# Cached-key scores by VectorE beside the prompt's attention, a split output projection, and an earlier routing table

## The reference

```
q, k = rope(rmsnorm(q)), rope(rmsnorm(k))            # 8 heads x 64
s = index_scores(qi, ki, wi); idx = top_k(s, 64)     # causal, per query
logits = (q . k[idx]) / 8;  p = softmax(logits)      # sample rows: k from cache_k[page_table] and the new key
y_att = p . v[idx]
y_ssm = gelu(y) * sigmoid(gelu(y) @ w_glu)
x = x + concat([y_ssm, y_att]) @ w_out
x = x + swiglu(rmsnorm(x)); x = x + pool_mixer(...); x = x + moe(top 2 of 8)
```

## Time and profile before

| | us |
|---|---|
| median of 3 runs | 1623.99 (1620.77 to 1626.13) |
| the profiled execution, device time | 1629.38 |
| the profiled execution, span in the trace | 1627.2 |
| PE busy | 1556.8 (96%) |
| DVE busy | 1256.8 (77%) |
| ACT busy | 987.8 (61%) |
| POOL busy | 115.0 (7%) |

### The profile page before, as it was taken

How to read it: one execution, slowest core, us unless ns; L and a number is a source line. 1 busy time by engine, 2 the same in 40 slices (tenths; PEclk the granted TensorE clock), 3 DMA queues, 4 the chain that set the end, 5 groups by cost and what they waited for, 6 DMA issues and landing times.

```text
span 1627.2 us, 23220 instructions
## 1 busy us (share of the span) xinstructions
PE 1556.8 (96%) x7648; PEld 1249.3 (77%) x7648; DVE 1256.8 (77%) x1670; ACT 987.8 (61%) x1305; POOL 115.0 (7%) x157
## 2 busy tenths in 40 slices
PE   6998988989999689999999999999999999999998
PEld 5664564789999567888888888888888888888886
DVE  8978820155544669989989889989988988988986
ACT  5111442144443157777777777778778778777774
POOL 1377510000000000000000000000000000000000
PEclk9998879999999889999999999999999999999999
DMA  6401125345445429999999999999998998999992
GB/s 226 154 26 53 56 84 153 107 142 179 156 143 169 157 78 332 373 343 332 365 348 325 369 357 319 364 357 319 369 371 303 367 372 311 362 367 335 345 358 98
DMA packets 212891, 420.83 MB, mean 259 GB/s; under 512 B 10233, under 2 KB 56469, under 8 KB 212572
## 3 DMA queue, kind: packets, MB, share of 16 engines
q1 hardware_dynamic: 211542, 414.37, 71.5%
q10 hardware_dynamic: 622, 3.45, 0.5%
q0 software_dynamic: 672, 2.32, 0.4%
HBM read 417.50 MB, written 3.07 MB: 258 GB/s over the span
## 4 chain that ended last, share of the span: by engine, by line
PE 83%; DVE 3%; ACT 1%; issue 1%; DMA 1%; SPq 1%; DVEq 0%; ACTq 0%
PE bank L1281 19%; PE bank L1280 19%; PE bank L1276 19%; PE bank L1139 3%; PE bank L1136 3%; PE bank L1140 3%; PE bank L1119 2%; PE bank L1301 2%; PE bank L1151 1%; PE bank L1155 1%; PE bank L1154 1%; PE bank L1239 1%; PE bank L866 1%; PE bank L1316 1%; PE bank L1056 1%
## 5 line engine op out<-in xcount | busy, mean ns | idle before, releaser
L2093 DVE TENSOR_TENSOR split<-raw_w,split 128x1024 fp32r<-128x1024 f32 x672 | 787.5, 1219 | 36.0 <-ACT split L1645 32.5
L1645 ACT ACTIVATE split<-raw_w 128x1024 fp32r<-128x1024 f32 x672 | 688.5, 1060 | 121.7 <-PE bank L1276 120.8
L1276 PE MATMUL bank<-split,xgr 128*128 128x512 f32 x896 | 357.5, 399 | 1.0 <-DVE xgr L2157 1.0
L1281 PE MATMUL bank<-split,xgr 128*128 128x512 f32 x896 | 353.5, 395 | 0.0
L1280 PE MATMUL bank<-split,xgr 128*128 128x512 f32 x896 | 353.3, 394 | 0.0
L1281 PEld LDWEIGHTS bank<-split,xgr 128*128 128x128 f32 x896 | 168.7, 188 | 39.5
L1276 PEld LDWEIGHTS bank<-split,xgr 128*128 128x128 f32 x896 | 168.8, 188 | 38.8 <-issue 1.4
L1280 PEld LDWEIGHTS bank<-split,xgr 128*128 128x128 f32 x896 | 168.9, 188 | 37.6
L1276 PE MATMUL bank<-split,hbr 128*128 128x512 f32 x448 | 178.0, 397 | 0.0
L1281 PE MATMUL bank<-split,hbr 128*128 128x512 f32 x448 | 176.9, 395 | 0.0
L1280 PE MATMUL bank<-split,hbr 128*128 128x512 f32 x448 | 176.8, 395 | 0.0
(11 more groups left out here) (392 smaller groups left out, 1932.7 us busy)
## 6 DMA issues: line engine op xcount, KB each, us to landing
raw_w<-in_moe_gate SPq DMA_DIRECT2D x112, 1024.0 KB, 6.1
raw_w<-in_moe_up SPq DMA_DIRECT2D x112, 1024.0 KB, 6.7
raw_w<-in_moe_down SPq DMA_DIRECT2D x112, 1024.0 KB, 6.2
ring<-in_w_gate SPq DMA_DIRECT2D x11, 1024.0 KB, 5.2
ring<-in_w_up SPq DMA_DIRECT2D x11, 1024.0 KB, 7.5
ring<-in_w_down SPq DMA_DIRECT2D x8, 1408.0 KB, 6.3
ring<-in_w_in SPq DMA_DIRECT2D x5, 2048.0 KB, 9.3
ring<-in_w_out SPq DMA_DIRECT2D x2, 2048.0 KB, 7.9
```

The lines of the kernel that those rows point to most:

```text
L1276: first = mm(out, hi, place[:, s, 0, cols], start=start, stop=False)
L1281: last = mm(out, hi, place[:, s, 1, cols], start=False, stop=stop)
L1645: A(place[:, s, 0, :], raw_w[:, at:at + BLOCK], ACT.Copy).then_inc(sem("high_ready"), 1)
L2093: TT(place[:, s, 1, :], raw_w[:, at:at + BLOCK], place[:, s, 0, :].bitcast(F32), ALU.subtract).then_inc(sem("low_ready"), 1)
```

## The change

1. **Sample scores.** The 16 `cT` fills, ACT's copies and the 32 products of `key_logits` go. In their place `qrow` turns the 8 sample queries into rows (four small transposes in the middle of the indexer's dots), ACT and DVE split them into high and low (`q_rows`), and for each request b PE spreads row b over 128 partitions (fill `qB`: two fp32r products of 8 rows by 512 columns). DVE multiplies the two key pages, untransposed, by that bank, and sums over the 64 dimensions of a head (`tensor_reduce`) into `klog`. At the end PE adds four terms in bank 7: the index mask, the scores with the new keys (`kself`), and two products of `klog` with the identity. The requests stand in the middle of the prompt's attention: 0 to 2 ahead of `scale_rows(0)` on DVE, 3 to 5 ahead of `scale_rows(1)`, 6 and 7 ahead of `scale_rows(2)`.
2. **Page order.** All four homes hold keys first: K0 K1, `wout1`, K2, K3, then K4 to K7 as `keys_used` allows, then V0 to V7.
3. **Reordered values.** `value_rows(2)` moves behind the scores of t = 1 and the first three `qB`. The last multiplication of the gate moves from POOL to DVE, between the masks of t = 0 and t = 1.
4. **Split output products.** The output projection is done with split blocks like the feed-forward layer: eight blocks through `place`, 192 products for 128 MATMUL instructions, and its input split into `wx` (high), `u_low` and `a_low`.
5. **Tables during the gather.** The slot table and the two register loads move ahead of `gathered_low(0)`; the gate and expert tables stay behind the first splits.

```
-    f += logits(0) + [("v", 2)] + logits(1) + probs_T(0) + [("att", 0)] + logits(2)
-    f += [("kt", t) for t in range(TC)] + [("attT", 0)] + probs_T(1) + [("att", 1)]
-    f += probs_T(2) + [("attT", 1), ("att", 2), ("attT", 2)]
-    for b in range(NB):
-        f += [("cT", b, 0), ("cT", b, 1)]
+    f += logits(0) + logits(1) + ["kself"] + spread(0, 1, 2) + [("v", 2)] + probs_T(0) + [("att", 0)] + logits(2)
+    f += spread(3) + [("kt", t) for t in range(TC)] + [("attT", 0)] + probs_T(1) + spread(4, 5) + [("att", 1)]
+    f += probs_T(2) + [("attT", 1)] + spread(6, 7) + [("att", 2), ("attT", 2)]
...
             for b in range(NB):
                 if b == 2:
                     load_unit(len(MIXER_UNITS) - 1)
-                if b >= 2:
-                    filled(sp, ("cT", b - 2, 1))
-                load_pages(b, "cache_k", kb, "ck")
-                if b < 2:
-                    load_pages(b, "cache_v", value_home(b), "cv")
-            for b in range(2, NB):
+                if b >= 4:
+                    sp.wait_ge(sem("keys_used"), b - 3)
+                load_pages(b, "cache_k", "ck")
+            for b in range(NB):
                 if b < 4:
-                    filled(sp, ("cT", b + 4, 1))
+                    sp.wait_ge(sem("keys_used"), b + 5)
...
+                if kind == "qB":
+                    out = open_fill(name)
+                    one = pick8[0:NB, t:t + 1].to_broadcast([NB, P])
+                    mm(out[:, :], one, q_rows[0:NB, 0, :], start=True, stop=False)
+                    mm(out[:, :], one, q_rows[0:NB, 1, :], start=False, stop=True).then_inc(full(name), 1)
...
             mask_logits(0)
+            TT(yv, ga, yv, ALU.mult).then_inc(sem("ssm_out"), 1)
             mask_logits(1)
+            def key_logits(b):
+                filled(dve, ("qB", b))
+                dve.wait_ge(sem(f"ck_in{b % 4}"), 32 * (b // 4 + 1))
+                TT(kprod.rearrange("p (g n) -> p g n", g=2), page_home(b),
+                   ps(("qB", b))[:, :].unsqueeze(1).to_broadcast([P, 2, 512]), ALU.mult).then_inc(free(("qB", b)), 1)
+                emptied(dve, ("qB", b))
+                nc.vector.tensor_reduce(klog[:, :, b * H:(b + 1) * H], kprod.rearrange("p (g h d) -> p g h d", g=2, h=H),
+                                        AX.X, ALU.add).then_inc(sem("keys_used"), 1)
+            for b in (0, 1, 2):
+                key_logits(b)
             scale_rows(0)
             mask_logits(2)
...
+                pe.wait_ge(sem("ff_low_ready"), co + 1)
                 for c in range(C):
-                    last = mm(out[:, 0:T], w[:, c, (co % 4) * P:(co % 4) * P + P], uT[:, c, :] if c < 4 else h3[:, c, :],
-                              start=(c == 0), stop=(c == C - 1))
+                    begun = mm(out[:, 0:T], w[0][:, c, :], wx[:, c, :], start=(c == 0), stop=False)
+                    mm(out[:, 0:T], w[0][:, c, :], low_in, start=False, stop=False)
+                    last = mm(out[:, 0:T], w[1][:, c, :], wx[:, c, :], start=False, stop=(c == C - 1))
...
+            pass_table(pslot[:, 0:PASSES, :], cand, slot_v)
+            n_pass = dve.value_load(exp_i[0:1, PASSES:PASSES + 1], min_val=NE, max_val=PASSES)
+            n_last = dve.value_load(exp_i[0:1, PASSES + 1:PASSES + 2], min_val=NE - 1, max_val=PASSES - 1)
             gathered_low(0)
```

More of the change, by code:

```diff
@@ L265 @@
 FF_BLOCKS = 2 * FT
+OUT_BLOCKS = C
 DOWN_CUTS = [(0, 8), (8, 16), (16, FT)]
@@ L993, in _ @@
                     continue
+                if name == "qrow":
+                    emptied(pe, ("qe", 3))
+                    out = open_fill(name)
+                    for c in range(4):
+                        last = nc.tensor.transpose(out[0:NB, c * P:(c + 1) * P], qT3[:, c, NP_:T], ident)
+                    last.then_inc(full(name), 1)
+                    continue
                 _, t, h = name
@@ L1019, in _, with sample_logits @@
                 last.then_inc(full(("glu", co)), 1)
-            emptied(pe, ("ke", 3))
-            for name in [n for n in FILLS if n[0] in PROMPT_FILLS]:
-                kind, t = name[0], name[1]
+            def sample_logits():
+                slog = ps("slogit")
+                emptied(pe, "sscore")
+                mm(slog[0:64, 0:SK], const("rsel")[32:40, :], sc[32:40, 2, 0:SK], start=True, stop=False)
+                emptied(pe, "kself")
+                mm(slog[0:64, PAST:SK], kself[32:40, :], ones[32:40, 0:1], start=False, stop=False)
+                pe.wait_ge(sem("keys_used"), NB)
+                for g in range(2):
+                    last = mm(slog[0:64, g * P:(g + 1) * P], klog[:, g, :], ident, start=False, stop=(g == 1))
+                last.then_inc(full("slogit"), 1)
+            emptied(pe, ("ke", 3))
+            for name in [n for n in FILLS if n[0] in PROMPT_FILLS or n in PROMPT_FILLS]:
+                if name == "kself":
+                    pe.wait_ge(sem("sample_q"), 1)
+                    out = open_fill(name)
+                    for c in range(4):
+                        last = mm(out[32:40, 0:64], kT3[:, c, NP_:T], qall3[:, c, :], start=(c == 0), stop=(c == 3))
+                    last.then_inc(full(name), 1)
+                    continue
+                kind, t = name[0], name[1]
+                if kind == "qB":
+                    if t == 0:
+                        pe.wait_ge(sem("q_rows_high"), 2)
+                        emptied(pe, "qrow")
+                    out = open_fill(name)
+                    one = pick8[0:NB, t:t + 1].to_broadcast([NB, P])
+                    mm(out[:, :], one, q_rows[0:NB, 0, :], start=True, stop=False)
+                    mm(out[:, :], one, q_rows[0:NB, 1, :], start=False, stop=True).then_inc(full(name), 1)
+                    continue
                 nq = QN[t]
-                if name == ("logit", 1, 0):
+                if name == ("pT", 0, 0):
                     value_rows(2)
+                if name == ("attT", 2):
+                    sample_logits()
                 if kind == "kt":
@@ L1600, in ff_high, with out_ready @@
                   ).then_inc(sem("ff_high_ready"), 1)
-            for n in range(FF_AHEAD):
-                ff_high(n)
-            squares(1, lambda c: emptied(act, ("wout", c)))
+            def out_ready(c):
+                n = c + FF_AHEAD
+                if n < OUT_BLOCKS:
+                    out_high(n)
+                else:
+                    ff_high(n - OUT_BLOCKS)
+                emptied(act, ("wout", c))
+            squares(1, out_ready)
             root(1)
@@ L2023, in ff_low @@
                    high.bitcast(F32), ALU.subtract).then_inc(sem("ff_low_ready"), 1)
-            for n in range(FF_AHEAD):
-                ff_low(n)
             for c in range(C):
+                n = c + FF_AHEAD
+                if n < OUT_BLOCKS:
+                    out_low(n)
+                else:
+                    ff_low(n - OUT_BLOCKS)
                 add_residual("wout", c)
```

199 lines of the change are left out of this document (121 added, 78 removed).

## The result

The changed kernel takes **1610.09 us** (median of 4 runs, 1606.85 to 1611.21), the kernel before in the same session 1624.7 (4 runs). The ratio is 0.9914, 95% interval [0.9893, 0.9934]: faster by 0.9%, about 15 us. Forecast were 1597 us, with 1588 to 1607 as the range. The sign was right and the size about half.

What follows compares the result with a forecast made beforehand. PE was taken to bound all three touched stages, with DMA arrivals between. Terms -20.0 + 0.8 - 5.9 - 2.0 = -27.1 took the profiled 1629.38 to 1602.3 us, by the median 1597, range 1588 to 1607.

Steps and rivals of the forecast that it cites:

- part 1: Sample's scores, moved to DVE: ready at 247.8 us in place of 267.78, a gain of 20.0 us.
- Value rows from 206 to 213.1: PE's value rows of t = 2 start once the sixth score's bank of t = 1 is free, taking 7.05 us.
- `qrow`: Four added transposes ahead of the state outputs delay PE, costing 0.8 us.
- `wout1` at 214, K2 at 223: SP's queue: `wout1` issued near 214 us, after the value rows and including 0.8 of delay; K2 lands near 223.
- the rule for a transfer behind another: SP's queue: `wout1` lands 8.1 us after issue, K2 1.35 us behind it, as w_up came behind w_gate.
- The block behind it: PE, from score 3 of t = 2 to the end of that t's products: 223.7 to 246.8 us.
- PE stays at the lower clock: Prompt's attention: standing still about 5 us for K2 slows PE's products by 4 to 6 us, total 1602; chance 17%.
- Closing products: PE's five last products of the sample's scores take 1.0 us, ending at 247.8 us.
- The output projection: 192 split products take 26.4 us in place of 32.11, 3.6 at the lower clock; with a pause gone, -5.9 us.
- The tables: Slot table and register loads fit into 2.95 us before the gather, removing PE's wait before the first scatter: -2.0 us.
- DVE becomes the bound: Sample's scores: DVE's product and sum forms cost far more, making the kernel slower, 1630 at 4.3 us each; chance 3%.
- K2 is not held: SP's queue: K2 lands 3 to 5 us after issue despite `wout1`, scores ready 4 us earlier, total 1593; chance 12%.

Runs made afterwards that it cites:

- second profile of before: The kernel before the change, unedited, profiled once more: 1623.89 us in one run, with a span of 1621.8 us.
- filled pause: The changed kernel with the sixth score product of t = 1 done five times over, so PE works through its 1.2 us pause: 1606.63 us, one run.
- experiment 1: The changed kernel with SP issuing K2 and K3 ahead of the second half of the output weights: 1599.39 us, ratio 0.9848 to the kernel before.
- experiment 2: The changed kernel with the value rows of t = 2 back between the scores of t = 0 and t = 1: 1596.74 us, ratio 0.9831 to before.
- experiment 5: The changed kernel with the slot table and the two register loads back behind the gather: 1608.16 us, ratio 0.9896 to the kernel before.
- experiment 7: The changed kernel with the output products not split, 128 products of raw weights as before: 1615.33 us, ratio 0.9932 to the kernel before.

## Why the prediction was wrong

**The step that failed is the size of part 1, the sample's scores: -20.0 forecast, -12.5 measured between the two profiled executions (68.44 to 55.90), -11.9 against the second profile of before.** The mechanism, `wout1` behind the value rows and K2 behind `wout1`, was right; its terms were taken at the full clock. The first of them to fail is the price of the value rows behind PE's pause: 7.05 us forecast, 9.67 measured.

- *Value rows from 206 to 213.1.* Measured 207.79 to 217.46. They started 1.8 us later: 0.8 was `qrow`'s own forecast, and PE had no wait left behind its pause but 3.4 us of work of its own (the last score, `kself` and three `qB`, 204.38 to 207.79), where the forecast let the bank of the sixth score decide. From `kself` on, that work took 2.8 us, and 2.1 with the pause filled. And the rows took 9.67 us. The filled pause shows the cause of the 2.6 us. The forecast had PE's pause in its own figures (it let the value rows wait for the sixth score's bank) and still carried 7.05 over.
- *`wout1` at 214, K2 at 223.* Measured 217.49 and 226.77. The distance is 9.3 us, as forecast: the rule for a transfer behind another (7.9 us for `w_out`, K2 some 1.3 behind it) held. That K2 follows `w_out` is also what the Trainium skill's "DMA: Bandwidth & Descriptors", section "Queues, rings and completion order", would have for the semaphore; no run here separates the order of the semaphores from the bandwidth that the two share.
- *The block behind it.* Score 3 of t = 2 began at 228.04, 1.3 us behind DVE's start, as worked out. From there to the end of the products of t = 2 the forecast has 23.1 us (223.7 to 246.8), measured 25.5 (to 253.51). From the pause to about 237 PE ran at the lower clock (12 transposes 2.82 us, not 1.53). This is the rival "PE stays at the lower clock", which had 17%; of its 4 to 6 us, 2.4 came. It looked for the lower clock only behind the stall for K2; the part ahead of it, under the value rows, is in no rival.
- *Closing products.* 1.0 forecast, 2.2 measured, and at the lower clock: 1.11 us for two of 257 columns that took 0.64 before.

From 248.6 (the 247.8 with `qrow`'s 0.8) to 255.7 that is 7.1 us: 3.5 up to K2, 2.4 in the block, 1.2 in the closing products.

**The output projection** was forecast at 26.4 us and took 25.1, so -5.9 looks confirmed: between the two first profiles the stretch shrank by 6.9. But 1.7 of those were the lower clock at the start of the old projection, which the second profile of before does not have. The edit is worth 5.25 us, by the undone kernel and by that profile alike. The forecast had taken its 3.6 us of low clock for granted in both kernels; neither the changed kernel's trace nor the second profile of before has it. It was 1.7 us too long on the old side and 1.3 on the new (26.4 against 25.1); that -5.9 came near 5.25 is because the two nearly cancel, which is luck.

**The tables** were forecast at -2.0 and are worth nothing. The wait in front of the first scatter went as forecast (the earlier trace rows had 2.44; the changed kernel has none), but the 2.95 us of cover belonged to an execution with the router at the lower clock. The register loads took 1.61 us, not the 1.2 that was estimated; the slot table took 1.3 as estimated. In the kernel without the split, where the router ran slowly again, the cover came back: gather to scatter took 13.5 us, not 16.2. The prediction asked what hides the tables and did not ask whether its cover was at the same clock as the rest.

**`qrow`** was put at +0.8; the first score product starts 0.5 us later than in the first trace of before (199.81 against 199.34), less than executions differ.

**From trace to median.** Between the two first profiles the span fell by 22.4 us, 4.7 less than forecast; medians fell by 14.6. The first profile of before was 5.4 us above its median and the profile of the changed kernel 3.2 below its own. The forecast took the 5.4 off at the end, as a constant; 5.0 of them lay in two stages that the change touches (1.7 and 3.3), at a clock that the changed kernel's trace does not have there, so that much of the 22.4 is no gain of the change. Against the second profile of before the changed kernel's span is 17.0 us shorter: 11.9 from the scores, 5.25 from the output projection, 0.7 each from the start and the feed-forward stretch, less 0.9 in router and loop and 0.7 in softmax and values, which the forecast had unchanged.

Of the other rivals, "DVE becomes the bound" did not happen (pairs of 2.5 us, PE's wait for DVE behind the third request 0.4 us), and "K2 is not held" is excluded by experiments 1 and 2. With K2 not held the prediction put 1593; measured are 1599 and 1597. One sum of the prediction is off without consequence: by its own terms DVE's rival gives 1627 at 4.3 us an instruction, not 1630. The cheap correction, one number in SP's loop or one name in the list of fills, makes the change worth 1.5 to 1.7% instead of 0.9.

## What to carry to other kernels

When a fill is moved in PE's order, follow not only who reads it but which transfer its end releases, and what stands behind that transfer in the same queue: here one move delayed K2's pages, and all behind them, by ten microseconds. A short wait of PE can cost twice, itself and the lower clock under the work behind it (here 1.2 and 2.6 us), so a duration read at one clock must not be carried behind a new pause. Before a cost is hidden in a gap of the profile, or a slow start is used as a base, look whether the gap belongs to an execution at the lower clock; a second profile of the same kernel tells.

## What the runs showed of the hardware

- A PE pause of 1.20 us was followed, some 2 us after its end, by 6.8 us at a granted clock of 0.50 (products of 512 columns 0.39 to 0.62 us, sixteen value-row products 9.5 to 9.8 us), in the changed kernel and in experiments 1, 5 and 7. With the pause filled it did not happen.
- The granted clock at one place of one kernel differs between executions: eight output products 3.81 or 2.12 us, twenty-four router transposes 5.10 or 2.82. Together that is 5 us of 1625.
- DVE: a product of 128x1024 with PSUM and repetition, and a sum of 1024 elements into 16, each took 1.22 us; the loads of the pass counts took 1.61 us in which DVE does nothing else (1.79 with the loop entry, experiment 5).
- The order on one queue: two pages of 0.25 MB issued 1.1 us behind a transfer of 2 MB were usable 9.3 us after the issue of the latter, against 7.9 us for the 2 MB itself (changed kernel).
